# One decoder layer: up projection by seven block products, up and down in two phases, joined forget logs

## What is computed

```python
def _merge_and_ffn(x, o_sb, o_fx, g_sb, g_fx, w_o, g_ffn, w_up, w_down):
    merged = g_sb * o_sb.reshape(B, L, W_Q) + g_fx * o_fx.reshape(B, L, W_Q)
    x = x + jnp.einsum('blm,md->bld', merged, w_o)
    h = _rms_norm(x, g_ffn)
    u = jnp.square(jax.nn.relu(jnp.einsum('bld,df->blf', h, w_up)))   # 2048 -> 8192
    return x + jnp.einsum('blf,fd->bld', u, w_down)                   # 8192 -> 2048

def _forgetting(q, k, v, cum_q, cum_k, q_pos, k_pos):                 # 16 heads
    z = jnp.where(k_pos[None, :] <= q_pos[:, None], z + cq - ck, -jnp.inf)
    p = jax.nn.softmax(z, axis=-1)
```

## Time and profile before

| | us |
|---|---|
| runs | 3491.46, 3488.50, 3484.49 (median 3488.5) |
| the profiled execution | 3489.46 |
| its span, first to last instruction | 3487.9 |
| output projection | 1760 to 1947 |
| norm, to Ln and Exp | 1947 to 1964 |
| up and down, eight chunks | 1964 to 3470 |
| turning and storing the result | 3470 to 3488 |

### The profile page before, as it was taken

How to read it: one execution, slowest core, us unless ns; L and a number is a source line. 1 busy time by engine, 2 the same in 40 slices (tenths; PEclk the granted TensorE clock), 3 DMA queues, 4 the chain that set the end, 5 groups by cost and what they waited for, 6 DMA issues and landing times.

```text
span 3487.9 us, 69078 instructions
## 1 busy us (share of the span) xinstructions
PE 3321.1 (95%) x25913; PEld 3154.6 (90%) x25913; DVE 1593.6 (46%) x2155; ACT 1329.4 (38%) x1837; POOL 342.7 (10%) x619
## 2 busy tenths in 40 slices
PE   5999999999999989987799899999999999999998
PEld 4999999999999988763389799999999999999998
DVE  4224666654444458887732433333333333333333
ACT  4224555554445447666621321312121222222221
POOL 0111111111111122223300000000000000000000
PEclk8999999999999999999999999999999999999999
DMA  4443333333333338779953223233333333333232
GB/s 150 115 116 104 98 95 95 99 99 99 91 107 107 96 102 290 256 262 353 333 188 85 60 85 97 84 97 84 96 84 96 84 96 84 96 84 96 84 96 85
DMA packets 481508, 430.02 MB, mean 123 GB/s; under 512 B 22129, under 2 KB 420338, under 8 KB 480258
## 3 DMA queue, kind: packets, MB, share of 16 engines
q1 hardware_dynamic: 441410, 311.74, 30.7%
q0 software_dynamic: 40032, 117.38, 10.0%
HBM read 405.56 MB, written 23.50 MB: 123 GB/s over the span
## 4 chain that ended last, share of the span: by engine, by line
PE 88%; DVE 4%; DMA 3%; issue 2%; ACT 2%; POOLq 1%; SPq 1%; POOL 0%; ACTq 0%; DVEq 0%
PE ps L630 26%; PE ps L632 26%; PE ps L631 26%; PE ps L828 3%; PE ps L836 2%; PE ps L837 1%; PE ps L761 1%; DVE pg_lo L1355 1%; DMA pg<-in_cache_sb_v_dram 1%; PE ps L674 1%; DMA pg<-in_cache_fox_v_dram 1%; DVE n_t L1382 1%; ACT pg_hi L1262 1%; POOLq L382 1%; PE ps L684 0%
## 5 line engine op out<-in xcount | busy, mean ns | idle before, releaser
L630 PE MATMUL ps<-h_hi,w_hi 128*128 128x260 f32 (+1 forms) x2592 | 758.2, 293 | 13.3 <-DVE h_lo L1355 10.5
L630 PE MATMUL ps<-m_hi,w_hi 128*128 128x260 f32 x2560 | 728.4, 285 | 27.2 <-DVE m_lo L1355 10.1
L632 PE MATMUL ps<-h_lo,w_hi 128*128 128x260 f32 (+1 forms) x2592 | 737.4, 284 | 0.0
L631 PE MATMUL ps<-h_hi,w_lo 128*128 128x260 f32 (+1 forms) x2592 | 737.1, 284 | 0.0
L632 PE MATMUL ps<-m_lo,w_hi 128*128 128x260 f32 x2560 | 726.5, 284 | 0.0
L631 PE MATMUL ps<-m_hi,w_lo 128*128 128x260 f32 x2560 | 725.3, 283 | 0.0
L1018 ACT ACTIVATE w_hi<-w_raw 128x2048 fp32r<-128x2048 f32 x225 | 429.8, 1910 | 738.3 <-PE ps L632 731.1
L1355 DVE TENSOR_TENSOR w_lo<-w_raw,w_hi 128x2048 fp32r<-128x2048 f32 x225 | 515.7, 2292 | 350.4 <-ACT w_hi L1018 345.6
L630 PE MATMUL ps<-u_hi,w_hi 128*128 128x260 f32 x2048 | 578.1, 282 | 5.7 <-ACT r_sb L1311 5.7
L631 PE MATMUL ps<-u_hi,w_lo 128*128 128x260 f32 x2048 | 577.7, 282 | 0.0
L632 PE MATMUL ps<-u_lo,w_hi 128*128 128x260 f32 x2048 | 577.4, 282 | 0.0
(11 more groups left out here) (236 smaller groups left out, 4008.0 us busy)
## 6 DMA issues: line engine op xcount, KB each, us to landing
w_raw<-in_w_in_dram SPq DMA_DIRECT2D x81, 1024.0 KB, 5.9
w_raw<-in_w_up_dram SPq DMA_DIRECT2D x64, 1024.0 KB, 6.4
w_raw<-in_w_down_dram SPq DMA_DIRECT2D x64, 1024.0 KB, 5.3
w_raw<-in_w_out_dram SPq DMA_DIRECT2D x16, 1024.0 KB, 5.9
kraw<-kT_dram POOLq DMA_DIRECT2D x32, 264.0 KB, 3.0
vraw<-out_dram POOLq DMA_DIRECT2D x32, 256.0 KB, 3.3
mg_dram<-mg POOLq DMA_DIRECT2D x32, 256.0 KB, 2.3
pg<-in_cache_sb_k_dram SPq DMA_DIRECT2D x32, 256.0 KB, 4.0
```

The costliest lines, as they stand in the source:

```text
L630: pe.matmul(out, whi, xhi, start=first, stop=False)
L631: pe.matmul(out, wlo, xhi, start=False, stop=False)
L632: return pe.matmul(out, whi, xlo, start=False, stop=last)
```

## The change

**Up in groups of two slabs.** 32 groups take the place of 64 slabs. The weights of a group are four quarter blocks a11, a12 (first slab, k 0 to 7 and 8 to 15), a21, a22 (second slab); the tokens four blocks b11, b12 (k 0 to 7, first and second half of the tokens), b21, b22. Seven products of quarter blocks make the four quarters of the result, with sums of blocks on both sides. POOL makes the four weight sums of each group in `sums` and `last_sum` (in place where it can), and once, at the start, the four token sums. ACT and DVE split seven quarter blocks of weights a group (1024 elements a partition) in place of two slabs of 2048, and, once, seven token blocks of 2080 elements a partition into `b_hi` and `b_lo`. The weight parts have four half-slots in `w_hi` and `w_lo` (`SLOT`); the product order on PE is 1, 6, 2, 5, 7, 3, 4, into three PSUM banks a group, two sets of them. DVE adds up the banks by way of `u_p1`, `u_p16`, `u_p165`, and Relu and square make `u_out`.

**Two phases.** All of up runs ahead of all of down. SP stores `u_out` of each group to `u_dram`, and in the down phase loads 1024 features at a time into `u_st`, which ACT and DVE split into one of two buffers `ub`. x2 is written to DRAM after the output projection, normed in place, and loaded again as `xd` for the additions of down.

**Start of up.** No up slab is split ahead during the output projection, and PE's first product waits for whole token blocks.

**Forget logs.** The high and the low part stand in one tile, `nck2`, at partitions 0 and 32, `sel` is filled at both places, and one matmul takes the place of two.

Some semaphores are joined, and tiles of the late part get addresses by hand.

```diff
+ORDER = (1, 6, 2, 5, 7, 3, 4)
+AT = {o: s for s, o in enumerate(ORDER)}
+SLOT = {1: 0, 6: 1, 2: 2, 5: 3, 7: 0, 3: 1, 4: 2}
...
+            def up_load(g):
+                p = g[1]
+                first, second = (wup_v[:, :, bass.ds(g[0] * (4 * P) + (p * 2 + i) * P, P)] for i in range(2))
+                split, summed = ready(sp, count(g, 7, -7), count(g, 4, -4))
+                wait(sp, a_lo, split)
+                wait(sp, a_sum_ok, summed)
+                sp.dma_start(u_raws[p][0][:, :, :], first).then_inc(up_ld[p], 16)
+                sp.dma_start(u_raws[p][1][:, :, :], second).then_inc(up_ld[p], 16)
+            def up_store(g):
+                p = g[1]
+                two = u_dram[bass.ds(g[0] * 4 + 2 * p, 2)].rearrange("m p t -> p m t")
+                sp.wait_ge(u_ok, count(g, 3, 3))
+                sp.dma_start(two, u_out[p][:, :, :]).then_inc(u_sv[p], 16)
...
+            sp.wait_ge(evac_v, 32 + FREE_DENSE)
+            sp.dma_start(x2_dram, x2T[:, :, :]).then_inc(x2_sv, 16)
+            sp.wait_ge(w_lo_ok, S_WO + KT)
+            up_load((0, 0))
+            sp.wait_ge(b_sum, 4)
+            sp.wait_ge(b_lo_ok, 7)
+            up_load((0, 1))
+            with sp.Fori(0, NU // 2 - 1) as j:
+                for p in range(2):
+                    up_load((j + 1, p))
+                    up_store((j, p))
...
+            sp.wait_ge(u_sv[0], 32)
+            sp.wait_ge(u_sv[1], 32)
+            stage(0)
+            for q, done in ((0, 4), (1, 6)):
+                sp.wait_ge(x2_sv, 16)
+                sp.wait_ge(p_ok, 7 * (NU - 1) + done)
+                sp.dma_start(xd[:, 8 * q:8 * q + 8, :], x2_dram[:, 8 * q:8 * q + 8, :]).then_inc(x2_ld, 16)
+            up_store((last, 1))
...
+            def sums(g):
+                p = g[1]
+                raw_1, raw_2 = u_raws[p]
+                a11, a21, a22 = raw_1[:, 0:8, :], raw_2[:, 0:8, :], raw_2[:, 8:16, :]
+                s1, s2 = (t[:, :, :] for t in a_sum)
+                loaded, first, second, summed = ready(pool, count((g[0], 0), 16, 32), count(g, 7, -6), count(g, 7, -4),
+                                                      count(g, 4, 2))
+                wait(pool, up_ld[p], loaded)
+                wait(pool, a_lo, first)
+                pool.tensor_tensor(s1, a21, a22, ALU.add).then_inc(a_sum_ok, 1)
+                pool.tensor_tensor(a21, a11, a21, ALU.subtract).then_inc(a_sum_ok, 1)
+                wait(pool, a_lo, second)
+                pool.wait_ge(a_sum_ok, summed)
+                pool.tensor_tensor(s2, a22, a21, ALU.subtract).then_inc(a_sum_ok, 1)
+            def last_sum(g):
+                a12 = u_raws[g[1]][0][:, 8:16, :]
+                split, summed = ready(pool, count(g, 7, 4), count(g, 4, 3))
+                pool.wait_ge(a_lo, split)
+                pool.wait_ge(a_sum_ok, summed)
+                pool.tensor_tensor(a12, a12, a_sum[1][:, :, :], ALU.subtract).then_inc(a_sum_ok, 1)
...
+            pool.wait_ge(m_lo_ok, 4)
+            sums((0, 0))
+            pool.wait_ge(y_ok, 2)
+            pool.tensor_tensor(b_t[:, :, :], part(0, 1), part(0, 0), ALU.subtract).then_inc(b_sum, 1)
+            pool.wait_ge(y_ok, 3)
+            pool.wait_ge(b_sum, 1)
+            pool.tensor_tensor(part(0, 1), part(8, 1), part(0, 1), ALU.subtract).then_inc(b_sum, 1)
+            pool.wait_ge(b_lo_ok, 2)
+            pool.tensor_tensor(b_t[:, :, :], part(8, 1), b_t[:, :, :], ALU.subtract).then_inc(b_sum, 1)
+            pool.wait_ge(b_lo_ok, 4)
+            pool.wait_ge(b_sum, 3)
+            pool.tensor_tensor(part(8, 0), part(8, 0), b_t[:, :, :], ALU.subtract).then_inc(b_sum, 1)
+            last_sum((0, 0))
+            sums((0, 1))
+            last_sum((0, 1))
+            with pool.Fori(1, NU // 2) as j:
+                for p in range(2):
+                    sums((j, p))
+                    last_sum((j, p))
...
-                        pe.matmul(out, sel[:, :], nck_hi[:, c0:c0 + wd], start=False, stop=False)
-                        mm = pe.matmul(out, sel[:, :], nck_lo[:, c0:c0 + wd], start=False, stop=not diag)
+                        mm = pe.matmul(out, sel[:, :], nck2[:, c0:c0 + wd], start=False, stop=not diag)
...
+            def product(g, o, bank, first, normed=False):
+                pe.wait_ge(a_lo, count(g, 7, {1: 2, 6: 3, 2: 4, 5: 4, 7: 5, 3: 6, 4: 7}[o]))
+                if normed:
+                    pe.wait_ge(b_lo_ok, TOKENS.index(o) + 1)
+                hi, lo = stationary(o)
+                for k in range(KT // 2):
+                    mm = split3(ps[:, bank, 0:HQ], hi[:, k, :], lo[:, k, :], b_hi[:, AT[o], k, :], b_lo[:, AT[o], k, :],
+                                first and k == 0, k == KT // 2 - 1, not first)
+                mm.then_inc(p_ok, 1)
+            def up(g, normed=False):
+                a, b, c = g[1], 2 + g[1], 4 + g[1]
+                wait(pe, r_ok, count(g, 2, -3))
+                product(g, 1, a, True, normed)
+                wait(pe, c_ev, count(g, 5, -6))
+                product(g, 6, b, True, normed)
+                pe.wait_ge(p1_cp, count(g, 1, 1))
+                product(g, 2, a, False, normed)
+                pe.wait_ge(c_ev, count(g, 5, 1))
+                product(g, 5, b, False, normed)
+                wait(pe, c_ev, count(g, 5, -5))
+                product(g, 7, c, True, normed)
+                pe.wait_ge(c_ev, count(g, 5, 2))
+                product(g, 3, b, False, normed)
+                pe.wait_ge(c_ev, count(g, 5, 3))
+                product(g, 4, c, False, normed)
...
+            def high(g, o):
+                wait(act, p_ok, count(g, 7, {1: -2, 6: -1, 2: 0, 5: -3, 7: 1, 3: 2, 4: 3}[o]))
+                if o in (1, 2, 4):
+                    act.wait_ge(up_ld[g[1]], count((g[0], 0), 16, 32))
+                else:
+                    act.wait_ge(a_sum_ok, count(g, 4, {5: 1, 7: 2, 6: 3, 3: 4}[o]))
+                act.activation(stationary(o)[0], source(o, g[1]), ACT.Copy).then_inc(a_hi, 1)
...
+            for o in (5, 1, 6, 2):
+                high((0, 0), o)
+            for o in TOKENS[:4]:
+                token_high(o)
+            def up(g, nxt, tokens=()):
+                a, p = g[1], g[1]
+                act.wait_ge(p_ok, count(g, 7, 1))
+                wait(act, c_ev, count(g, 5, -1))
+                act.activation(u_p1[:, :], ps[:, a, 0:HQ], ACT.Copy).then_inc(p1_cp, 1)
+                for o in tokens[:1]:
+                    token_high(o)
+                high(g, 7)
+                for o in tokens[1:]:
+                    token_high(o)
+                high(g, 3)
+                if tokens:
+                    act.wait_ge(b_lo_ok, 7)
+                act.wait_ge(p_ok, count(g, 7, 3))
+                wait(act, u_sv[p], count((g[0], 0), 8, 0))
+                act.activation(u_out[p][:, 0, 0:HQ], ps[:, a, 0:HQ], ACT.Relu).then_inc(r_ok, 1)
+                high(g, 4)
+                act.wait_ge(r_ok, count(g, 2, 1))
+                act.activation(u_out[p][:, 0, 0:HQ], u_out[p][:, 0, 0:HQ], ACT.Square).then_inc(r_ok, 1)
+                if nxt is not None:
+                    for o in (5, 1, 6, 2):
+                        high(nxt, o)
...
+                    dve.tensor_copy(sel[0:NH, :], pick)
+                    dve.tensor_copy(sel[LOW:LOW + NH, :], pick).then_inc(sel_ok, 1)
...
+            dve.wait_ge(nrm["rs2"], 2)
+            dve.wait_ge(x2_sv, 16)
+            normed(0, 0)
+            normed(0, 1)
+            low((0, 0), 5)
+            low((0, 0), 1)
+            token_low(1)
+            normed(8, 1)
+            normed(8, 0)
+            low((0, 0), 6)
+            low((0, 0), 2)
+            for o in TOKENS[1:4]:
+                token_low(o)
...
+                for o in tokens[:1]:
+                    token_low(o)
+                low(g, 7)
+                dve.wait_ge(p1_cp, count(g, 1, 1))
+                dve.wait_ge(p_ok, count(g, 7, 2))
+                dve.tensor_tensor(u_p16[:, :], u_p1[:, :], b, ALU.add).then_inc(c_ev, 1)
+                for o in tokens[1:]:
+                    token_low(o)
+                low(g, 3)
+                dve.wait_ge(p_ok, count(g, 7, 4))
+                dve.tensor_tensor(u_p165[:, :], u_p1[:, :], b, ALU.add).then_inc(c_ev, 1)
+                low(g, 4)
                 if nxt is not None:
-                    split_lo(nxt)
+                    low(nxt, 5)
+                dve.wait_ge(p_ok, count(g, 7, 5))
+                dve.wait_ge(c_ev, count(g, 5, 2))
+                wait(dve, u_sv[p], count((g[0], 0), 8, 0))
+                if tokens:
+                    dve.wait_ge(b_lo_ok, 7)
+                dve.tensor_tensor(u22, u_p165[:, :], c, ALU.add).then_inc(c_ev, 1)
+                if nxt is not None:
+                    low(nxt, 1)
+                relu_square(u22, 3)
+                dve.wait_ge(p_ok, count(g, 7, 6))
+                dve.tensor_tensor(u12, u_p1[:, :], b, ALU.add).then_inc(c_ev, 1)
+                if nxt is not None:
```

(39 more changed lines are left out.)

404 lines of the change are left out of this document (232 added, 172 removed).

## The result

The changed kernel takes **3435.0 us** (median, 3432.9 to 3437.7) where the kernel before took 3487.9 in the same comparison: a ratio of 0.9849, interval 0.9832 to 0.9866, some 53 us less. The profiled execution has a span of 3436.2 us against 3487.9.

A forecast was written before the change was run, and what follows sets the result against it. PE's matmul count bounds the kernel; 3487.9 - 92.0 - 15 - 10 + 15 + 34 + 10 = 3429.9 us of span, forecast 3431 us as a median, range 3390 to 3485.

The forecast's parts named there:

- Matmuls, -92.0: Up: 168 matmuls a group in place of 192 for a pair of slabs, over 32 groups, 92.0 us less.
- Steady stall, +15: Steady up groups: DVE's two-input operations and POOL's sums exclude each other, 0.5 us for 30 groups; bounds 0 and +70.
- the hand schedule: Steady up group timed: with exclusion, addition u22 ends some 0.5 us after product 4 would want its bank.
- totals (20.3 against 20.1): Steady up group: 9.9 us of DVE's two-input operations plus 10.4 of POOL's sums, against PE's 20.1.
- Start, +34: Start of up: token and weight sums in a row end group 1 near 2063 against 2029.4; bounds +20 and +46.
- Seams, -15: Seven seams between chunks and the first chunk's inner one go, 15 us less; bounds -17.5 and -10.
- border, +10: From up to down: DVE's additions and next weight split wait for x2's reload, 10 us more; bounds +5 and +16.
- Forget logs, -10: Forget-log heads: one of two `sel` matmuls goes, 0.64 us in each of 16 heads; bounds -11 and -5.
- Port-bound: Rival, steady up groups: DVE and POOL serialize more, 21.5 us a group, 3458 us (3446 to 3485); chance 0.21.
- DVE starved: Rival, steady up groups: low part 7 waits for four POOL sums, 6.2 us a group, 3602 us; chance 0.15 with similar hold-ups.
- the signs that would make me wrong: Sums over 3.5 us, low parts as long as a sum, weights after 5 us of a group, start ending after 2075.

The follow-up runs named there:

- the two border experiments: Changed kernel with VectorE taking x2 by halves and splitting the second down slab earlier: ratio 0.9854; the same with the second chunk's activations behind the weights: 0.9821.
- the experiment: Changed kernel with forget logs as in the kernel before (two tiles, two matmuls a part, one copy into the selector): ratio 0.9874, 9 us more.

## Why the prediction was right, point by point

The direction and the size held: 3431 forecast, 3435 measured. The terms did less well than the sum.

- **Matmuls, -92.0.** Right: 30 groups gave -86.2, and the other two groups' 5.8 lie in the start. Wrong is the sum: the start was measured to the end of group 1 against four slabs, so it held these 5.8 already, and I counted them twice.
- **Steady stall, +15.** Measured 0.6. The mechanism was there, the place was right (u22 behind low parts 4 and 5), and the size was not. The step that failed is the hand schedule that put u22 0.5 us too late: in the group shown u22 ended at 2322.66, ahead of the seventh product, which began 2.87 us before its u21 at 2326.12. I took sums of 2.6 us (alone they take 2.4), and counted the relu squares among the excluding operations; in the steady windows none of them started while a sum ran (0.42 us each), so the runs don't show whether they exclude. Above all I set totals (20.3 against 20.1) against PE, where the ring of waits decides, and that has by the estimate above some 3.8 us of room.
- **Start, +34.** Measured +39.7. Relative to the last addition of the output projection, product 1 came at 39.9 us (forecast 40), product 6 at 64.1 (forecast 65), and the request for group 1 at 81. The forecast was close with two errors inside: token sums alone took 4.4 to 4.6 us, not 5.2, while the second was shut out for 7.6 us by DVE. I had expected POOL to shut out DVE there for up to 5 us. The term that was mis-sized is the end: group 0 ended at 102.7, not 88, since u22 stood in DVE's queue behind a low part that waited for the load, and that load took 11 us, not 8 (for the same two megabytes in the steady groups I had reckoned with some 10). PE waited 11.1 us with product 4 ready but for its bank.
- **Seams, -15, and border, +10.** The old seams (17.4 by the earlier trace rows and the table) went altogether. The new one cost 14.4, 4.4 over the term and inside its bounds. I had the wait for x2, and missed that the next stage and two weight slabs queue behind the same 6 MB, so that a second wait follows the first: the two border experiments show it, the first by moving the wait, the second by removing it. That down's slabs would be slower (11.515 against 11.45, 4.1 us) stands in no term; its cause is open.
- **Forget logs, -10.** 10.9 by the experiment. The traces of before and after show only -5.0 up to the last addition, since that part differs by more than this from one execution to the next.
- **Rivals.** Port-bound didn't come: the group stayed at PE's 20.13. DVE starved didn't either. Two more sums a group cost 3.2 us, over the 2.4 at which I said that it decides, but not in its way: no low part waited for a row of sums (the longest took 3.38 us), the ring had grown past PE's period. The lower end that I gave port-bound, 3446, doesn't follow from 20.6 us a group, which would make 3431. Of the signs that would make me wrong, low parts as long as a sum were there one by one (3.36 us), and weights landing after 5 us of a group (POOL waited some 0.7 us a group for them); both were hidden by the same room.

In sum, measured against forecast: +5.8 counted twice, -15 of stall that didn't come, +5.7 in the start, +4.4 at the border, +4.1 in down's slabs, +5.0 ahead of up, -2.4 of old seams and -1.3 in the tail. That is +6.3, from 3429.9 of span to 3436.2. The size came out because errors of both signs met; that it came within 4 us was luck.

## What to carry to other kernels

A second engine's slow operations cost nothing here as long as the ring of waits that they close is shorter than the bound engine's period: add up the ring, not the engines' busy shares. Where that slack is absent, in a start or at a border between phases, the same operations cost time at once (9.5 us of the start came back with the token sums on VectorE), and a transfer or an operation queued ahead of what is due next costs its wait a second time. When an edit at a border moves nothing, look for the wait that came in place of the one removed before giving the border up.
